# A PEER decoder trunk on one core: VectorE adds three second rows of nearly every tile

## What is computed

```python
        q = (xb @ w_query).reshape(tb, PEER_HEADS, 2, PEER_KEY_DIM // 2)
        s = jnp.einsum('thpd,pnd->thpn', q, sub_keys).astype(jnp.float32)
        top_s, top_i = lax.top_k(s, k)
        cand_s = top_s[:, :, 0, :, None] + top_s[:, :, 1, None, :]
        cand_i = top_i[:, :, 0, :, None] * PEER_N_KEYS + top_i[:, :, 1, None, :]
        best_s, best_j = lax.top_k(cand_s.reshape(tb, PEER_HEADS, k * k), k)
        idx = jnp.take_along_axis(cand_i.reshape(tb, PEER_HEADS, k * k), best_j, axis=-1)
        gate = jax.nn.softmax(best_s, axis=-1)
        u = expert_u[idx]
        act = jax.nn.gelu(jnp.einsum('thkd,td->thk', u, xb).astype(jnp.float32))
        w = (gate * act).astype(xb.dtype)
        return jnp.einsum('thk,thkd->td', w, expert_v[idx])
```

## Time and profile before

| | us |
|---|---|
| median of 3 runs | 1953.07 |
| lowest and highest | 1942.4 and 1957.02 |
| the profiled execution | 1964.85 |
| its span, first to last instruction | 1963.0 |

### The profile page before, as it was taken

One profiled execution on the slowest core, in us unless ns is written; L12 is line 12 of the kernel. 1 busy time (PEld: TensorE's weight loads), 2 busy tenths in 40 slices (PEclk: granted clock), 3 DMA queues, 4 the chain that ended last, 5 costly groups with the idle time before them and its releaser, 6 DMA issues.

```text
span 1963.0 us, 14465 instructions
## 1 busy us (share of the span) xinstructions
PE 1520.7 (77%) x4023; PEld 708.2 (36%) x4023; DVE 1103.2 (56%) x2713; ACT 360.6 (18%) x916; POOL 1062.1 (54%) x1111
## 2 busy tenths in 40 slices
PE   8999986676796764789887775887876848667678
PEld 3477635334332221334333422333333413222223
DVE  2433235757477455765776566676764656555541
ACT  1032112111132111131221121221211211111111
POOL 1110014655666666656676466666665556566664
PEclk9955597887899988889999797899988979988999
DMA  5210226998899988899999898999998789888896
GB/s 175 89 43 5 81 74 222 413 356 337 329 377 350 382 351 342 306 381 389 416 418 416 308 387 310 392 415 413 384 400 333 286 334 360 343 341 340 339 375 254
DMA packets 184126, 616.74 MB, mean 314 GB/s; under 512 B 19275, under 2 KB 20811, under 8 KB 184054
## 3 DMA queue, kind: packets, MB, share of 16 engines
q0 software_dynamic: 152064, 553.72, 72.1%
q1 hardware_dynamic: 31990, 62.17, 8.5%
HBM read 614.77 MB, written 1.05 MB: 314 GB/s over the span
## 4 chain that ended last, share of the span: by engine, by line
PE 33%; DVE 17%; issue 14%; DMA 12%; POOL 12%; another core or an unknown queue 11%; ACT 1%; DVEq 0%; SPq 0%; POOLq 0%
PE bank L882 14%; POOL arena L603 12%; DMA arena<-peer_u,idx 9%; PE bank L681 8%; DVE arena L1592 6%; PE bank L783 3%; DMA arena<-peer_v,idx 2%; PE bank L856 2%; PE bank L755 1%; PE bank L744 1%; DVE best_j L1540 1%; DMA wring<-gla_w_in 1%; DVE pairs L1574 1%; DVE pairs L1577 1%
## 5 line engine op out<-in xcount | busy, mean ns | idle before, releaser
L882 PE MATMUL bank<-arena 128*128 128x512 f32 x1944 | 962.3, 634 | 337.9 <-DMA arena<-peer_v,idx 159.1
L1592 DVE CUSTOM_DVE_ANT_0 arena<-arena,bank 128x1024 f32<-128x1024 f32 x528 | 626.2, 1217 | 283.3 <-DMA arena<-peer_u,idx 201.7
L603 POOL DMA_INDIRECT arena<-peer_u,idx x528 | 523.6, 992 | 403.1 <-DVE dots L1592 173.6
L882 PEld LDWEIGHTS bank<-arena 128*128 128x128 f32 x1944 | 365.0, 199 | 896.1 <-issue 474.7
L603 POOL DMA_INDIRECT arena<-peer_v,idx x528 | 507.8, 962 | 247.7 <-issue 151.9
L681 PE MATMUL bank<-wring,hT 128*128 128x512 f32 (+5 forms) x604 | 265.4, 593 | 11.7 <-issue 9.1
L1187 ACT ACTIVATE arena<-con,wgt 128x128 f32<-128x128 f32 x486 | 156.2, 391 | 472.1 <-issue 195.7
L681 PEld LDWEIGHTS bank<-wring,hT 128*128 128x128 f32 (+1 forms) x604 | 109.4, 183 | 160.9 <-issue 153.3
L1176 ACT ACTIVATE gl<-dots 128x16 f32<-128x16 f32 x33 | 7.1, 215 | 403.8 <-issue 273.6
L568 POOL TENSOR_TENSOR small<-small,con 128x1 f32<-128x1 f32 (+2 forms) x12 | 9.1, 761 | 127.2 <-DVEq L1358 78.7
L581 POOL COPY arena<-gws 128x288 f32 x16 | 8.9, 554 | 117.9 <-PE bank L744 101.2
(11 more groups left out here) (155 smaller groups left out, 1005.5 us busy)
## 6 DMA issues: line engine op xcount, KB each, us to landing
wring<-gla_w_in SPq DMA_DIRECT2D x12, 2048.0 KB
arena<-peer_u,idx POOLq DMA_INDIRECT x528
arena<-peer_v,idx POOLq DMA_INDIRECT x528
wring<-gla_w_out SPq DMA_DIRECT2D x4, 2048.0 KB
wring<-peer_w_query SPq DMA_DIRECT2D x4, 2048.0 KB
wring<-attn_w_in SPq DMA_DIRECT2D x2, 2048.0 KB
wring<-attn_w_out SPq DMA_DIRECT2D x2, 2048.0 KB
gws<-peer_w_query SPq DMA_DIRECT2D x2, 2048.0 KB, 10.3
```

The costliest lines, as they stand in the source:

```text
L603: nc.gpsimd.indirect_dma_start(out=ring[:, slot, :], out_offset=None, in_=table.rearrange("l e d -> (l e) d"), in_offset=bass.IndirectOffs ...
L882: last = nc.tensor.matmul(yacc[:, 512 * i:512 * i + 512], wdiag[:, k, :], vrow[:, v_slot(g, k), 512 * i:512 * i + 512], start=first, stop= ...
L1592: v.tensor_tensor_reduce(out=rows, in0=rows, in1=xnow, scale=1.0, scalar=0.0, op0=ALU.mult, op1=ALU.add, accum_out=dots[:, g % 2, k:k + 1] ...
```

## The change

`by_vector` no longer asks whether a mixer runs beside the tile. Every tile from 2 to 31 is shared:

```diff
         def by_vector(g):
 
-            return SHARE if mixer_turn(g + 1)[0] and mixer_turn(g + 1)[1] < len(TENSOR_AT) else ()
+            return SHARE if 1 < g < TILES - 1 else ()
 
         def by_tensor(g):
             return [k for k in range(TOPK) if k not in by_vector(g)]
```

## The result

| us | before | after |
|---|---|---|
| median (10 runs each) | 1951.94 | 1962.38 |
| lowest and highest | 1942.4, 1961.23 | 1953.9, 1975.68 |
| the profiled execution | 1964.85 | 1975.68 |
| its span | 1963.0 | 1973.8 |

The ratio is 1.0075, with a 95% interval of 1.0044 to 1.0105: the changed kernel is 14.6 us slower by the ratio, 10.4 by the medians, and the two profiled executions stand 10.8 us apart. The interval leaves out 1, so the changed kernel is slower, by 0.4 to 1.1%.

A forecast was written before the change was run, and what follows sets the result against it. A plain turn was bounded by GpSimd's 40 us of gathers plus a 9.4 us pause behind VectorE's late chain. Terms 0.7 + 7.4 - 3.7 = +4.4 us gave a 1957 us median; forecast's own range 1940 to 1972, with rivals 1925 to 1988.

The forecast's parts named there:

- The price of an add: Each new VectorE add holds GpSimd's gathers 0.82 us; 39 us for 48 adds, 2.5 us a turn.
- the case of 61 us: Every new add holds GpSimd for its whole 1.28 us, 61 us in all.
- the cover, the pause: GpSimd's wait of about 9.4 us in a plain turn shrinks when gathers come later, hiding the adds' hold.
- the port is the whole story: Rival: held gathers come late and no pause gives way, +36 us, 1989 us; chance 0.28.
- 4: turns 17 and 25: The following turns' long pause takes up their 2.5 us: 0; end +5.
- 5: the end: The last 21 mixes on TensorE do not move: 0; ends 0 and +1.3 us.
- Step 1: Turns 8, 9, 26, 28 to 31, with the long pause: 7 x 0.1 = +0.7 us; ends -17 and +17.
- the relief rival: Turns 3 to 5 give back 15.5 us, the pause shrinks 2.5 us in seven turns: -33, 1920 us; chance 0.24.
- Step 2: Turns 6, 7 and 27, where nothing hides the adds: 3 x 2.5 = +7.4 us; ends 0 and +14.
- the long chain: Sign of error: VectorE's 17.6 us expert-choosing chain appearing in turns 3 to 7, moving the result 3 to 5 us a turn.
- step 3: Turns 3 to 5 under TensorE, nine mixes fewer, only turn 4 above GpSimd's pace: -3.7 us; ends -15.5 and +10.
- VectorE overloaded: Rival: VectorE overloaded by the adds, with 27 + 4 us of work in 49; given no chance.

The follow-up runs named there:

- the run without block 1: The changed kernel with tiles 2 to 8 given back to TensorE, 27 new adds staying, on a late chip: ratio 0.9982 (0.9923 to 1.0041) to the kernel before.
- the adds made small: The changed kernel with its 48 new adds cut to 8 of 1024 columns: 1765.94 against 1764.11 us for the kernel before, 1.0006.
- the adds from PSUM: The kernel before plus 48 extra VectorE adds, 47 reading one input from PSUM: 1765.35 against 1763.9 us, 1.0005.
- the chain spread out: The kernel before with VectorE's expert-choosing chain cut at its waits and put between dots: 1.0042, again 1.0027, both on prompt chips.

## Why the prediction was right, and where its steps were not

The forecast of 1957 us stands beside 1962.38, and the likeliest case was the one that came. But where the sum said +4.4 us, the profiled executions stand 10.8 apart, and the ratio gives 14.6. That the total landed so near is in part luck: the hold of an add was put too high and the share of it that comes through too low, and the largest misses of single steps have opposite signs.

**The price of an add: 0.82 us forecast, 0.59 measured on the late chip, 0.54 on a prompt one.** This term was mis-sized. It laid the whole difference between two windows of about 128 gathers on 12 adds and called the rest (norm instructions) small. All 48 adds hold GpSimd for 28.2 us, not 39. The kind of cost was right and is shown: two inputs from SBUF cost it (1.24%), one input from PSUM does not (0.05%). The full length of an add is never lost (at most 1.05 of 1.28 us on the prompt chip), since a gather under way when the add begins goes on; the case of 61 us is refuted. The prediction quoted the rule that the one that comes second is held. The traces show only half of that: a gather that begins under an add is held, an add that begins under a gather is not (63 such adds, all of 1.28 us).

**How much of it reaches the end.** I let 8.1 of 39 us through. In fact 10 to 15 of 28.2 came through on the late chip, and nine tenths or so on the prompt ones. The two pages of the late chip balance: the gathers took 28.2 us more, GpSimd's idle time before them fell from 650.8 to 633.1 us, 17.7 less, and 10.5 remain of the 10.8. So the cover, the pause, exists as I said and gives way, by more than the hold in turns 28 to 31 of this one trace and by less over the whole kernel, and only on a chip that has it. The evidence that I gave for it was weak, though: 49.41 beside 49.32 us compared turns 20 to 22, which carry mixer work, with plain turns. On the prompt chip, with no pause, the same turns of the kernel before take 46.7 and 40.3 us, so equal lengths on the late chip did not show that a pause had hidden the adds. On a prompt chip the change costs 1.4%, with the rival "the port is the whole story" right in kind and too high in size (39 us for 25). Its condition was "a fixed pause"; what makes it true there is no pause at all, which I had not thought of.

**The steps**, from the turn lengths of the two profiled executions, with the caution above:

| step | forecast | measured |
|---|---|---|
| 1: turns 8, 9, 26, 28 to 31 | +0.7 | -6.5 |
| 2: turns 6, 7 and 27 | +7.4 | +13.0 |
| 3: turns 3 to 5 | -3.7 | -1.0 |
| 4: turns 17 and 25 | 0 | +2.5 |
| 5: the end | 0 | +1.0 |
| the start to turn 2 | 0 | +2.0 |
| turns 10 to 16 (+3.8) and 18 to 24 (-4.0) | 0 | -0.2 |

Step 1 is the nearest to the relief rival: the restarts came at 48.2 us, between the forecast's 49.4 and the 47 at which relief would have been right. But the run without block 1 has 49.72 with the same work, so 1.5 us a turn lie within what two traces differ by, and -6.5 is no measured gain. Step 2 came out near its upper end, which was "each rises to 49.3": turn 27 at 49.0 in the change and also in the run without block 1, 44.3 before, and turns 6 and 7 at 98.0. And the long chain appeared in turns 5 to 7, which the prediction had named as a sign that it was wrong: step 2's term was the bare hold of the adds, 2.5 us a turn, and what came was longer turns with the long chain in them. This fits the mechanism that I wrote under the relief rival only (a relieved TensorE lets GpSimd stream on until it meets the long pause) and gave no term in the sum. That it is the cause is argued, not shown: on a prompt chip no such pause is there to be met, no run relieves TensorE without the adds on a late one, and the run without block 1 has part of the longer chain with TensorE not relieved there. In step 3 turn 4 fell from 53.0 to 49.5 us as said, but it is 49.1 in the run without block 1, where nothing relieves it, so the change need not be the reason; turn 5 gave 2.2 back.

**The rival of relief** fails on a prompt chip: 48 mixes less, with the adds made small, give 1.0006. TensorE was busy 128 us of 161 in turns 28 to 31 there, yet it waits for rows that GpSimd orders at its own pace. Nor did I cost what TensorE does with its free time: its matmuls became longer, 627 to 661 ns, and gave half of the relief back.

**VectorE overloaded**, the rival without a chance, is refuted by the adds from PSUM, on a prompt chip.

**Open.** Why VectorE's chain waits so long on some chips and not on others, with the same kernel, and on a late chip in some turns and not in others; whether the chain spread out would win there; and how much of turns 6, 7 and 27 is the relief's and how much the adds'. Of the kernels that compute everything, none was shown to be faster than the kernel before.

## What to carry to other kernels

Before work is moved to VectorE beside an engine that issues indirect gathers, look where its inputs lie: here an instruction with two SBUF inputs held GpSimd for about 0.55 of its 1.28 us in the mean, one with an input from PSUM for nothing, though VectorE had room for both. Taking work from an engine that waits for data in the bounding stretch gained nothing, however busy it looked (80% here). And cover that one trace shows, such as a pause behind late signals, may be missing on the next chip: price a change without the cover too.

## What the hardware showed that I had not expected

- The same kernel takes 1764 us on three chips and about 1950 on at least one. Most plainly longer is a chain of short VectorE instructions beside streaming gathers: 5.6 us with hardly a wait, 17.6 with waits of up to 6. On the late chip the same chain is short in some turns and long in others.
- TensorE with less to do was clocked lower, with the adds or without them: over the whole kernel 0.895 with the change and 0.891 with the new adds made small, against 0.924 before, all on prompt chips. In turns 28 to 31 on a prompt chip the granted clock fell from 1.00 (2.4 GHz) to 0.86, a mix of the level of 2.4 and that of 1.2 GHz, when three mixes in sixteen were gone and TensorE waited longer for rows (L882's idle time went from 231.4 to 303.2 us over the whole kernel). Of 95 us of mixes removed, L882's busy time shows 45 saved on that chip and 35.5 on the late one. The Trainium skill (TensorE: Matmul & The Clock Gate, Part 1) names idling as what puts TensorE at half rate; these rows agree in direction.
- A gather under way is not lengthened by an add that begins beside it, nor is the add. Only a gather that begins under the add is, by what is left of the add less 0.12 to 0.14 us (77 of 77 in the change's trace on the prompt chip); the six there that began within 0.08 us of an add's start lost nothing.
